# Two transformer blocks on one core: most projections as three passes on high and low halves, a two-pass layer norm, and projections moved ahead of the attentions

## The reference, cut to what matters

```
for l in range(2):                                   # layers 0 and 1
    q, k, v, r, a_low, u, v_sgu = split_proj(x @ w_in[l])
    h = concat([gla_group(q, k, v, r, a_low, ...), sgu_group(u, v_sgu, ...)]) @ w_out[l]
    x = layer_norm(ALPHA * x + h, ...)
    h = mem_xattn(x, mem, wq, wk, wv, wo)            # (x@wq), (mem@wk), (mem@wv), softmax, @wo
    x = layer_norm(ALPHA * x + h, ...)
    x = layer_norm(ALPHA * x + grouped_moe(x, ...), ...)
for layer in (even, odd):
    shift, scale, gate, ... = split(silu(c) @ ada_w[layer] + ada_b[layer], 6)
    h = rmsnorm(x, g) * (1 + scale) + shift
    x = x + gate * mixer(h)      # even: NSA and MoBA attention; odd: MLA and sliding-window (SWA)
    x = x + gate2 * grouped_moe_2(rmsnorm(x, g2) * (1 + scale2) + shift2, ...)
return rmsnorm(x, final_norm)
```

## Time and profile before

| | us |
|---|---|
| median of 3 runs | 2531.67 (2531.66 to 2540.68) |
| the profiled execution: device time / span | 2538.12 / 2536.3 |
| busy: PE / DVE / ACT | 2202.3 (87%) / 1510.3 (60%) / 1084.8 (43%) |
| mean granted clock of TensorE | 0.93 |

### The profile page before, as it was taken

The page is one execution under the profiler, slowest core; times in us unless marked ns, Lnnn a source line. Parts: engine busy times, 40 slices in busy tenths (PEclk is TensorE's granted clock), DMA queues, the critical chain, the costliest instruction groups (busy, mean ns, idle before and its releaser), DMA issues.

```text
span 2536.3 us, 25817 instructions
## 1 busy us (share of the span) xinstructions
PE 2202.3 (87%) x9464; PEld 1669.2 (66%) x9464; DVE 1510.3 (60%) x1922; ACT 1084.8 (43%) x1164; POOL 86.5 (3%) x82
## 2 busy tenths in 40 slices
PE   8999799898899959989788976999978677699996
PEld 4656488787475648878677746777753364577775
DVE  2653488787455357978724145878840224577876
ACT  1101276675110127766413214767730022476773
POOL 0110000000111000000000000000000000000000
PEclk9999799999899969999976997999989889699998
DMA  9664288798666418978640213888876221388883
GB/s 408 276 230 196 83 327 328 285 345 304 271 240 257 162 65 332 344 289 330 262 166 34 100 67 133 318 330 306 312 270 253 98 98 69 116 323 331 301 316 128
DMA packets 48680, 596.26 MB, mean 235 GB/s; under 512 B 5200, under 2 KB 7248, under 8 KB 8784
## 3 DMA queue, kind: packets, MB, share of 16 engines
q1 hardware_dynamic: 34560, 500.19, 52.4%
q0 software_dynamic: 8352, 59.77, 5.9%
q10 hardware_dynamic: 5680, 35.09, 3.8%
HBM read 591.89 MB, written 3.15 MB: 235 GB/s over the span
## 4 chain that ended last, share of the span: by engine, by line
PE 63%; issue 21%; DVE 8%; ACT 3%; DMA 3%; POOL 1%; DVEq 0%; ACTq 0%; POOLq 0%
PE bank L654 57%; PE bank L684 2%; PE bank L873 2%; DMA hi_ring<-in_ada 1%; POOL small L2141 1%; PE bank L884 1%; DMA x<-in_x_in 1%; DVE ring_parts L1497 1%; DVE work L1497 1%; DVE x L1497 1%; ACT hi_ring_parts L1157 1%; ACT work L1157 0%; DVE mix L1568 0%; DVE hi_ring L1838 0%; DVE work_parts L1497 0%
## 5 line engine op out<-in xcount | busy, mean ns | idle before, releaser
L1497 DVE TENSOR_TENSOR ring_parts<-ring,hi_ring_parts 128x2048 fp32r<-128x2048 f32 x384 | 860.3, 2286 | 107.6 <-ACT hi_ring_parts L1157 107.6
L1157 ACT ACTIVATE hi_ring_parts<-ring 128x2048 fp32r<-128x2048 f32 x384 | 724.1, 1914 | 140.4 <-PE bank L654 126.9
L654 PE MATMUL bank<-hi_ring_parts,xT_parts 128*128 128x512 f32 x1024 | 340.9, 405 | 48.5 <-DVE ring_parts L1497 48.5
L1157 ACT ACTIVATE work<-bank 128x512 f32<-128x512 f32 (+7 forms) x215 | 113.6, 531 | 621.5 <-PE bank L654 499.9
L654 PE MATMUL bank<-hi_ring_parts,work_parts 128*128 128x512 f32 x1024 | 328.7, 392 | 24.7 <-DVE work_parts L1497 24.7
L654 PE MATMUL bank<-hi_ring_parts,oT_parts 128*128 128x512 f32 x1024 | 331.4, 394 | 4.8 <-DVE ring_parts L1497 4.8
L654 PEld LDWEIGHTS bank<-hi_ring_parts,xT_parts 128*128 128x128 f32 x1024 | 199.5, 195 | 94.5 <-DVE ring_parts L1497 52.7
L654 PEld LDWEIGHTS bank<-hi_ring_parts,work_parts 128*128 128x128 f32 x1024 | 192.2, 188 | 69.9 <-issue 30.5
L654 PEld LDWEIGHTS bank<-hi_ring_parts,oT_parts 128*128 128x128 f32 x1024 | 192.4, 188 | 48.0 <-DVE ring_parts L1497 8.5
L654 PE MATMUL bank<-ring_parts,xT_parts 128*128 128x512 f32 x512 | 205.2, 401 | 0.0
L654 PE MATMUL bank<-ring_parts,oT_parts 128*128 128x512 f32 x512 | 199.6, 390 | 0.0
(11 more groups left out here) (189 smaller groups left out, 2161.1 us busy)
## 6 DMA issues: line engine op xcount, KB each, us to landing
ring<-in_weights SPq DMA_DIRECT2D x238, 2048.0 KB, 7.8
hi_ring<-in_ada POOLq DMA_DIRECT2D x48, 1024.0 KB, 11.2
hi_ring<-in_weights ACTq DMA_DIRECT2D x12, 2048.0 KB, 7.7
work<-in_vecs POOLq DMA_DIRECT2D x8, 1024.0 KB, 5.1
bias_rows<-work ACTq DMA_DIRECT2D x8, 256.0 KB, 4.0
work<-bias_rows ACTq DMA_DIRECT2D x2, 1024.0 KB, 7.6
params<-in_prm ACTq DMA_DIRECT2D x1, 1485.5 KB, 13.2
consts<-in_cst ACTq DMA_DIRECT2D x1, 1040.0 KB, 19.5
```

The source lines that it names most:

```text
L654: ins = nc.tensor.matmul(o, lhsT, rhs, start=start, stop=stop)
L1157: return nc.scalar.activation(o, i, f, **kw)
L1497: return v.tensor_tensor(o, a, b, op)
```

## The change

- 35 pieces of projections (11 in each of layers 0 and 1, 8 in e, 5 in o) run in three passes on high and low halves. ACT and DVE get a `split` of each half, placed by hand in their order; x and the attention outputs get high and low halves too. The `xk` and `xv` pieces, the compression weights `ck`, `cv` and the latent weights `up` stay in float32.
- The 24 gate columns of e join the piece `kw`, and `e.gates` is no product of its own.
- `layer_norm` multiplies (x - mean) by the gain ahead of the wait for POOL, and scales and adds the bias behind it.
- The modulation columns leave `hi_ring`, which the halves now need: a load has one column (512 KB), two are in flight (in `spare`), and the plan is spread anew.
- In e, `mq`, `mk`, `mv` run ahead of NSA, and the NSA and MoBA units are one loop; in o, `sq`, `sk` run ahead of the latent products, and the MLA and SWA units are one loop. The loop on ACT and DVE is a step longer for its outputs.

```diff
-ADA_EACH = 2
-ADA_AHEAD = 4
-ADA_PLAN = {"key": 3, "gate": 7, "mixed": 1, "out": 3, "query": 7, "xo": 3}
+ADA_AHEAD = 2
+ADA_PLAN = {"gate": 20, "mixed": 2, "out": 6, "query": 10, "xo": 10}
...
+        class Part:
+            def __init__(self, name, h):
+                m, n = PIECE_AT[name]
+                self.slot, self.full = m % RING, 16 * (m // RING + 1)
+                self.n = n + h + 1
+                self.free = SPLIT_HALVES[self.n - 1 - HI_RING] + 1 if self.n > HI_RING else 0
+                self.raw = ring[:, self.slot, h * HALF:(h + 1) * HALF]
+                self.hi = hi_ring[:, (self.n - 1) % HI_RING, :]
+                self.lo = ring_parts[:, self.slot, h * HALF:(h + 1) * HALF]
...
+            def split_piece(name):                                  # PE
+                pe.wait_ge(lo_ready, n + 2)
...
+            def moving(x_, w, T, at, n):
+                return [pair for c in range(DC) for pair in ((x_[0][:, c, t], hi(c)), (x_[0][:, c, t], lo(c)),
+                                                             (x_[1][:, c, t], hi(c)))]
...
+            def split(name):                                        # ACT
+                for h in range(2):
+                    part = Part(name, h)
+                    act.wait_ge(slot_full[part.slot], part.full)
+                    if part.free:
+                        act.wait_ge(halves_done, part.free)
+                    fn(part.hi, part.raw, ACT.Identity).then_inc(hi_ready, 1)
...
+            def split(name, halves=(0, 1)):                         # DVE
+                for h in halves:
+                    part = Part(name, h)
+                    dve.wait_ge(hi_ready, part.n)
+                    tt(part.lo, part.raw, part.hi, ALU.subtract).then_inc(lo_ready, 1)
...
                 eps(slice(0, 2), mv_[:, :, 1], 1.0, LN_EPS).then_inc(var_ready, 1)
+                vectors_loaded()
+                for h, c in enumerate(cols):
+                    for T in range(NT):
+                        (...)(v.scalar_tensor_tensor(
+                            out=x[:, T, c], in0=src[:, T, c], scalar=mv_[:, T, 0:1], in1=lnv[:, 0, c],
+                            op0=ALU.subtract, op1=ALU.mult))
                 rstd(2)
-                for T in range(NT):
-                    (...)(v.tensor_scalar(
-                        x[:, T, :], src[:, T, :], mv_[:, T, 0:1], stat_out[:, T:T + 1], ALU.subtract, ALU.mult))
-                vectors_loaded()
-                for h in range(2):
-                    step(tt(x[:, :, c], x[:, :, c], lnv[:, 0:1, c].broadcast_to([P, NT, 512]), ALU.mult))
-                    ins = tt(x[:, :, c], x[:, :, c], lnv[:, 1:2, c].broadcast_to([P, NT, 512]), ALU.add)
+                for h, c in enumerate(cols):
+                    for T in range(NT):
+                        ins = v.scalar_tensor_tensor(
+                            out=x[:, T, c], in0=x[:, T, c], scalar=stat_out[:, T:T + 1], in1=lnv[:, 1, c],
+                            op0=ALU.mult, op1=ALU.add)
...
                 tt(gg, gg, gE, ALU.subtract).then_inc(gla_g, 1)
-                modulation(l, ADA_PLAN["gate"])
+                for name in (f"{tg}.sv", f"{tg}.u"):
+                    for h in range(2):
+                        modulation(l, 3)
+                        split(name, (h,))
+                modulation(l, 3)
...
-                residual(f"{tg}.xo", l, ADA_PLAN["xo"])
+                split(f"{tg}.xo1")
+                residual(f"{tg}.xo", l, (1, 4, 3, 2))
...
-            adaptive_norm("e.turn0", 0, pr("norm_mix")[:, 0:8], 8, 0)
+            split("e.q")
+            adaptive_norm("e.turn0", 0, pr("norm_mix")[:, 0:8], 8, 0, second_x)
...
-            adaptive_norm("o.turn0", 1, pr("norm_mix")[:, 8:16], 8, 0)
+            split("o.c")
+            adaptive_norm("o.turn0", 1, pr("norm_mix")[:, 8:16], 8, 0, second_x)
+            split("o.sq")
...
             tell(rope_ready)
+            split("o.out0")
             dve.wait_ge(zeros_set, 3)
...
-            attention(numbered(mla_units(), ATT["mla"]))
             dve.wait_ge(bias_ready, 1)
-            attention(numbered(swa_units(), ATT["swa"]))
+            attention(numbered(mla_units(), ATT["mla"]) + numbered(swa_units(), ATT["swa"]))
+            split("o.out1")
```

More of the change, by code:

```diff
@@ L368, in program @@
         rt = cut(work, NS + 1920, 512)
-        swq = cut(work, NS, PAIRS, S)
+        swq = cut(silu_row, 0, PAIRS, S)
         swk = cut(work, NS + 7552, 2, S)
@@ L397, in program @@
         alow = sb("alow", S)
-        silu_row = sb("silu_row", D)[:, :]
-        ada_in = [hi_plain[:, j, :].rearrange("p (r k) -> p r k", r=ADA_EACH) for j in range(ADA_AHEAD)]
+        ada_in = [cut(spare, j * D, D) for j in range(ADA_AHEAD)]
         pad_w = cut(work, GL + 3072, 2 * NT, 8, 33)
@@ L1219, in turned_probs, with outputs @@
                                                   lambda t: t[0:kp, :].rearrange("p (a b) -> p a b", a=4)[:, 0:4:2, :])])
-                for k in range(len(units) + 2):
-                    if k < len(units):
+                def outputs(u):
+                    if u["last"]:
+                        banks.wait_full(act, u["o"])
+                        r = u["regions"]
+                        fn(u["dest"][0], psum[banks.jobs[u["o"]][0]][:, 0:r * P].rearrange("p (a b) -> p a b", a=r),
+                           ACT.Identity).then_inc(att_out, 1)
+                n = len(units)
+                for k in range(n + 4):
+                    if k < n:
                         exps(units[k])
@@ L1371, in _ @@
                 if l:
-                    turned(f"{l - 1}.turn3")
+                    split(f"{tg}.q")
+                    turned(f"{l - 1}.turn3", plain_xT)
+                    for q in range(DC // 2):
+                        x_hi(first_x[0], plain_xT, q, f"{l - 1}.turn3")
+                split(f"{tg}.v")
+                if l:
+                    whole(alow[0:GATE_RANK, :], f"{tg}.alow")
                 whole(gqT, f"{tg}.q", scale=0.125)
-                whole(alow[0:GATE_RANK, :], f"{tg}.alow")
+                if l == 0:
+                    whole(alow[0:GATE_RANK, :], f"{tg}.alow")
+                split(f"{tg}.r")
                 for T in range(NT):
@@ L1385, in _ @@
                 whole(decay, f"{tg}.dec", ACT.Exp)
+                split(f"{tg}.out0")
                 for T in range(NT):
@@ L1389, in _ @@
                     whole(xkT[:, 2 * j:2 * j + 2, :], f"{tg}.xk.{j}")
-                for q in (0, 2):
-                    whole(oT[:, 2 * q:2 * q + 2, :], f"{tg}.turn0.{q}")
+                    if j == 1:
+                        split(f"{tg}.out1")
+                turned_hi(f"{tg}.turn0", first_o[0])
+                split(f"{tg}.xq0")
+                split(f"{tg}.xq1")
                 def memory_values(q):
@@ L1432, in _ @@
                            for a in range(2)])
-            attention(numbered(nsa_units(), ATT["nsa"]))
-            for j in range(2):
-                whole(mq[:, 2 * j:2 * j + 2, :], f"e.mq.{j}", scale=0.125)
+            split("e.mv")
             act.wait_ge(zeros_set, 2)
@@ L1440, in _ @@
                                     for a in range(2)])
+            split("e.out0")
             for T in range(NT):
@@ L1545, in layer_norm, with residual @@
                 tell(vecs_used)
-            def residual(tag, l, loads):
+            def residual(tag, l, loads, ahead=None):
                 for j, (T, q) in enumerate(OUTS):
-                    modulation(l, 1 if j < loads else 0)
+                    if j == 2 and ahead:
+                        split(ahead)
+                    modulation(l, loads[j])
                     p_ = bank(f"{tag}.{T}.{q}")
@@ L2000, in _ @@
                 dve.wait_ge(mix_ready, l + 1)
-                turned(f"{tg}.turn0", oT)
-                residual(f"{tg}.out", l, ADA_PLAN["out"])
+                turned_lo(f"{tg}.turn0", first_o)
+                residual(f"{tg}.out", l, (3, 2, 1, 0), f"{tg}.xq0")
                 layer_norm(x)
                 tell_x()
-                turned(f"{tg}.turn1")
-                modulation(l, ADA_PLAN["query"])
+                turned_lo(f"{tg}.turn1", first_x)
+                for h in range(2):
+                    split(f"{tg}.xq1", (h,))
+                    modulation(l, 2)
+                for h in range(2):
+                    modulation(l, 2)
+                    split(f"{tg}.xo0", (h,))
+                modulation(l, 2)
                 attention(numbered(cross_units(f"{tg}.x"), ATT[f"{tg}.x"]))
-                residual(f"{tg}.xo", l, ADA_PLAN["xo"])
+                split(f"{tg}.xo1")
+                residual(f"{tg}.xo", l, (1, 4, 3, 2))
                 layer_norm(x)
@@ L2042, in _ @@
             dve.wait_ge(bias_back, 32)
-            attention(numbered(nsa_units(), ATT["nsa"]))
-            attention(numbered(moba_units(), ATT["moba"]))
+            for name in ("e.mk", "e.mv", "e.out0"):
+                split(name)
```

(4 more changed lines are left out.)

422 lines of the change are left out of this document (267 added, 155 removed).

## The result

The changed kernel takes 2607.51 us (median of 4 runs, 2603.35 to 2612.65), the kernel before 2534.71 beside it (4 runs, 2531.66 to 2540.68). The ratio is 1.0289, with a 95% interval of 1.0262 to 1.0316: 2.9% slower, where 2531 and a range up to 2562 were forecast. The span of the profiled execution is 2610.6 us against 2536.3: +74.3.

What follows compares the result with a forecast made beforehand. PE, busy 87% of the span, was taken to bound the kernel. Savings in projections and loops nearly cancelled waits for columns: terms sum to -0.2 us, which from the median 2531.67 gives 2531, range 2500 to 2562.

Steps and rivals of the forecast that it cites:

- layer 0 to turn2: Layer 0 up to `turn2`: 20.0 us later, with v starting at 48.6 where it started at 31.22.
- layer 1 to turn2: Layer 1 up to `turn2`: 8.3 us later, at 266.2 us from the layer's start where it was 257.9.
- clock: Whole kernel: 3 us lost to a lower granted clock behind the new stops, an estimate from 0 to 8.
- the reload, r: Modulation columns: time from a column's end to its buffer full again, 4.3 us alone, 5.6 beside weights, taken as 5.0.
- From there PE leads: Layer 1 from `mix` at 93.0 us on: PE's own work sets the time, until ten columns stand between DVE's residuals.
- the walk with r = 5.0: Layer 1 timed step by step with 5.0 us per column reload: `sv` at 51.2, `mix` at 93.0, `turn2` at 266.2.
- the reload is slow: Rival, chance 0.23: column reloads from 5.7 us on make the kernel slower than the bound; at 7.0 us, 2569.
- -4 in e and, taken as like, -4 in o: Attention loops: one merged loop saves two steps and a wait, adds an output step; 4 us less in each layer.
- the pass of 256 columns: Three-pass projections on PE: each pass of 256 moving columns takes 0.12 us, so 96 passes take 11.5.
- the norm: Two-pass layer norm: 3.3 to 3.7 us less at each norm that PE waits for.
- the splits that lie open: Two splits behind the norm, ahead of `e.turn0` and `o.turn0`: they cost 4.5 us at each place.
- v of layer 0: Layer 0's v projection waits for a column and a half: starts at 48.6 us, before at 31.22.

Runs made afterwards that it cites:

- e2: The changed kernel with every modulation column worked off by DVE, on two buffers loaded only once; sums set to 0.01; 2399.96 us.
- e6: The changed kernel with NSA and MoBA, and MLA and SWA, as two loops each again; 2604.36 us.
- e7: The changed kernel with attention outputs copied in float32 inside the loops and split into halves only behind them; 2596.29 us.
- e1: The changed kernel with no modulation columns at all (no loads, no DVE work; sums set to 0.01); 2367.94 us.
- e4: The kernel before with the two-pass layer norm alone; 2523.81 us, ratio 0.9956.
- e11: The changed kernel with layers 0 and 1 in float32, eight column buffers, outputs split behind loops, `e.q` and `o.c` split inside the norm; 2501.31 us.

## Why the prediction was wrong

Its sum put term by term beside the two traces, in us. The stretches lie between PE's marks (the rows above show those up to `e.turn0`), and add up to the +74.3 of the span:

```
                                   predicted   measured
layer 0 to turn2                    +20.0       +49.8   (330.73 and 280.95)
experts, start of layer 1            -0.5        -0.9
layer 1 to turn2                     +8.3       +38.0   (295.9 and 257.9 from alow and q on)
experts, start of e                  +2.5        +0.3
projections of e                    -12.9       -11.5
loop of e                            -4.0        +8.4
out of e                             -5.8        -5.7
experts, start of o                  +6.2        +4.7
projections of o, split of out0      -7.2        -7.4
loop of o                            -4.0        +4.0
out of o, rest                       -5.8        -5.3
clock                                +3          (in the rows above)
```

**The step that failed is the reload, r, and with it "From there PE leads".** r was taken as one number: "Half of these 2.7 on top of 3.9 gives 5.2 ... I take 5.0, in the middle: a stalled PE lets the weight queue rest." Alone a load lands in 3.5 (r = 4.0, near the 4.3 of the prediction), beside weights in 8.1 to 8.7 (r = 9.1 and not 5.6). Half the bytes of the 1 MB load did not land sooner. The 7.8 of the earlier trace rows was itself a median of three loads, 9.1, 5.0 and 7.8, of which the 5.0 had almost no weights beside it. A stalled PE did not let the queue rest either: PE takes a piece as soon as its halves are there, SP loads the next 2 MB in the same moment (`sv` of layer 0 starts at 86.20, the load at 87.15), and the columns that the next half stands behind load beside it. The median landing is 7.1 us up to 310, and 5.3 from 697 to 994.

What that did is seen in layer 1, stretch by stretch (us):

```
                 predicted   measured   without loads (e2)
alow to mix         93.0        99.4        77.1
mix to turn0        33.1        40.4        37.6
turn0 to xq         43.6        46.6        45.0
xq to xo            55.3        65.6        55.9
xo to turn2         41.2        43.9        30.8
sum                266.2       295.9       246.4
```

Up to `mix` the walk with r = 5.0 was nearly right: 6.4 us of the 29.7 are lost there (e6 and e7, the same program up to here, have `mix` at 100.4 and 100.8). The other 23.3 are lost where the prediction let PE lead and counted no wait for DVE until the residuals. From `xq` to `xo`, 10.3 us late, ten columns stand ahead of DVE's work on the cross attention, and its first maximum starts behind the last of them:

```profile
926.30 1.23 DVE L2021 CUSTOM_DVE_ANT_0 spare<-spare,silu_row 128x1024 f32<-128x1024 f32 x1 [6.75 <-DMA spare<-in_ada]
...
927.46 0.69 DVE L1746 TENSOR_REDUCE small<-bank 128x2 f32<-128x512 f32 x1
```

Without loads that stretch takes 55.9, what was predicted. From `mix` to `turn0` most of the 7.3 is there without loads too, and isn't explained by them. No single r mends the walk. With r = 7.5 its steps end near the measured `turn2` (295), but by luck: they put `sv` at 56, u at 82 and `mix` at 109, where 51.4, 73.2 and 99.4 were measured, and the excess there stands in for the waits behind `mix` that the walk leaves out. The rival "the reload is slow" named the right mechanism; its 2569 was still 38 us short.

Why half the bytes land no sooner is in part seen in the trace. A load of a column is 144 packets in the queue q0, in both kernels (0.52 MB now, 1.05 MB before): the change halved the packets and not their number. Where both queues move data they take turns, one for one. The rows are of 208 to 210.4 us, within the load shown above:

```profile
q1 hardware_dynamic: 50, 0.80, 78.0%
q0 software_dynamic: 48, 0.20, 19.9%
```

So a column beside weights gets a fifth of the bytes. The load also starts late: from 203.8, where it is issued, to 207.4 only packets of weights move, while alone the first packet comes 1.3 us after the issue (97.76). Why it starts late stays open. The Trainium skill (DMA: Bandwidth & Descriptors, "Queues, rings and completion order") says that a DMA engine goes round its queues by packets. The one-for-one turns above agree. It counts some 9 to 17 descriptors as one packet, though, and whether the profile's packets are those isn't shown here.

**The clock** was entered with +3, at most 8. Up to `turn2` of layer 1 alone the lower clock is part of 27 us more of PE's busy time than in e1. How much of that is the clock alone wasn't measured.

**The loops** are the second failed term: "-4 in e and, taken as like, -4 in o". That merging takes two steps off isn't borne out: with two loops (e6) each is 1.8 us shorter than merged. With the split behind, the merged loop of e is 8.2 us below before and that of o 0.5 above (e7). And the split of the outputs was counted as one step more at the end, when it is an operation on ACT and a wait of DVE in every step, with the bank held until it is done (16.6 and 3.5 us). Measured are +8.4 and +4.0 against -4 and -4, together 20.4 us.

**Right were** the pass of 256 columns, 0.12 us:

```profile
25.05 0.28 PE L707 MATMUL bank<-xT_parts,ring_parts 128*128 128x256 f32 x1
25.16 0.28 PE L707 MATMUL bank<-mix_parts,hi_ring_parts 128*128 128x256 f32 x1
25.28 0.28 PE L707 MATMUL bank<-xT_parts,hi_ring_parts 128*128 128x256 f32 x1
```

These three start 0.11 and 0.12 apart (71 of them 8.5 us, 0.120), each with a weight load of its own; the rule on weight loads of the Trainium skill (TensorE: Matmul & The Clock Gate, part 3, "What overlaps and what doesn't"), by which the prediction made it 0.213, does not hold here. Right were also, to about 1.5 us, the norm (e4), the splits that lie open ahead of `e.turn0` and `o.turn0`, the projections of e and o, the two `out`, v of layer 0 (48.6, measured 46.2) and the start of `sv` (51.2, measured 51.4).

## What to carry to other kernels

A stream that was hidden is hidden by its buffers: before its buffers are given to something else, price one reload beside the heaviest traffic that it will meet, not alone and not by bytes, and at every place where work waits behind it, not by one mean. A walk that ends at the right place proves little; its marks on the way have to be right too. A three-pass product saves TensorE a fifth of its time (10.9 for 13.8 us) only where the halves are ready early; here a late half cost its wait and, behind it, some microseconds at the lower clock. In a tight loop between three engines, put a conversion that only the next product needs behind the loop.

## What the runs showed that was not expected

Time in which DVE waits for POOL is not free: POOL's power took 2.90 us with DVE idle, 3.36 beside four operations of DVE (e4) and 4.87 beside the split of a half (e11).

A load of 512 KB beside 2 MB of weights lands as late (8.1 to 8.7 us) as one of 1 MB did (7.8 and 9.1), and in 3.5 without them. PE's passes of 256 columns start 0.21 apart, and not 0.12, at the start of the kernel (the clock's record begins only behind them, at 24.7 us) and again in `e.q`, from 1370.2 to 1372.8, where the granted clock is 0.50, its lower level of 1.2 GHz; from 1374 to 1380 it is 1.00 and they start 0.12 apart. The rows are of the start:

```profile
20.14 0.41 PE L707 MATMUL bank<-xT_parts,ring_parts 128*128 128x256 f32 x1
20.36 0.41 PE L707 MATMUL bank<-mix_parts,hi_ring_parts 128*128 128x256 f32 x1
20.57 0.41 PE L707 MATMUL bank<-xT_parts,hi_ring_parts 128*128 128x256 f32 x1
```

`sv` of layer 1 behind its wait of 10.85 us is alike: its passes of 512 columns start 0.43 apart up to 755, at a granted clock of 0.50, and 0.227 from 756 on, at 1.00.
